# One expert at a time on both column halves of TensorE: sums in PSUM, 20 MB of landing room, 2 MB transfers with 16 KB runs

## What is computed

```python
def moe(h, w_router, b_router, w_up, b_up, w_down, b_down):
    logits = (x @ w_router + b_router)
    top_vals, top_idx = lax.top_k(logits, TOP_K)             # 4 of 32
    combine = jnp.sum(one_hot(top_idx, N_EXPERTS) * softmax(top_vals)[..., None], axis=1)

    def expert(acc, xs):
        wu, bu, wd, bd, g = xs                               # wu 1024 x 2048, wd 1024 x 1024
        gu = x @ wu + bu
        gate, up = gu[:, :D_FF], gu[:, D_FF:]
        gate = jnp.minimum(gate, SWIGLU_LIMIT)
        up = jnp.clip(up, -SWIGLU_LIMIT, SWIGLU_LIMIT)
        glu = gate * jax.nn.sigmoid(SWIGLU_ALPHA * gate)
        y = ((up + 1.0) * glu) @ wd + bd
        return acc + g[:, None] * y, None
```

## Time and profile before

| | |
|---|---|
| median of 3 runs | 1152.67 us (1152.51, 1152.67, 1154.61) |
| profiled execution | span 1150.5 us from its first to its last instruction; the time around its span is not recorded for it; the median of the runs is 2.2 us above this span |
| moved | 459.15 MB, mean 399 GB/s |
| TensorE matmul busy | 1054.2 us (92%) |
| VectorE, ScalarE, GpSimd busy | 331.5, 176.1, 55.6 us |
| granted TensorE clock, mean | 0.985 |

### The profile page before, as it was taken

The page is one execution under the profiler, slowest core; times in us unless marked ns, Lnnn a source line. Parts: engine busy times, 40 slices in busy tenths (PEclk is TensorE's granted clock), DMA queues, the critical chain, the costliest instruction groups (busy, mean ns, idle before and its releaser), DMA issues.

```text
span 1150.5 us, 13989 instructions
## 1 busy us (share of the span) xinstructions
PE 1054.2 (92%) x5718; PEld 518.3 (45%) x5718; DVE 331.5 (29%) x613; ACT 176.1 (15%) x319; POOL 55.6 (5%) x92
## 2 busy tenths in 40 slices
PE   7999999999999999989899998989898989898986
PEld 6987699834434343424243433333434333343422
DVE  4675877412213112111120202120212121212125
ACT  4453145401101010101010101010101010000011
POOL 5050000300000000000000000000000000000000
PEclk9999999999999999999999999999999999999999
DMA  9988987799999999999999999999999999999995
GB/s 309 376 247 334 385 289 311 281 419 428 427 400 428 427 429 428 428 428 429 428 429 428 428 428 428 428 429 428 429 428 428 429 428 428 428 427 424 421 420 212
DMA packets 58658, 459.15 MB, mean 399 GB/s; under 512 B 4804, under 2 KB 17160, under 8 KB 28056
## 3 DMA queue, kind: packets, MB, share of 16 engines
q1 hardware_dynamic: 57256, 455.12, 95.6%
q0 software_dynamic: 1168, 2.81, 1.0%
q10 hardware_dynamic: 192, 0.66, 0.2%
HBM read 456.99 MB, written 1.57 MB: 399 GB/s over the span
## 4 chain that ended last, share of the span: by engine, by line
PE 61%; DMA 33%; DVE 2%; SPq 2%; issue 1%; ACT 1%; DVEq 0%; ACTq 0%
DMA ring<-in_w_down_dram 30%; PE ps L1862 17%; PE ps L1877 10%; PE ps L1798 6%; PE ps L1751 5%; PE ps L1762 5%; PE ps L1447 3%; DMA ring<-in_w_in_dram 2%; PE ps L1897 2%; PE ps L1791 1%; PE ps L1778 1%; DMA ring<-in_w_ada_dram 1%; PE ps L1504 1%; PE ps L1505 1%; PE ps L1673 1%
## 5 line engine op out<-in xcount | busy, mean ns | idle before, releaser
L1862 PE MATMUL ps<-ring,arena 128*64 128x512 f32 x1664 | 364.5, 593 | 14.6 <-DMA ring<-in_w_up_dram 14.5
L1877 PE MATMUL ps<-ring,arena 128*64 128x512 f32 x896 | 210.8, 626 | 54.6 <-DMA ring<-in_w_down_dram 54.6
L1862 PEld LDWEIGHTS ps<-ring,arena 128*64 128x64 f32 x1664 | 121.0, 137 | 241.6 <-issue 239.2
L1877 PEld LDWEIGHTS ps<-ring,arena 128*64 128x64 f32 x896 | 72.5, 144 | 192.6 <-issue 173.5
L1305 DVE TENSOR_TENSOR arena<-ps,arena 128x512 f32<-128x512 f32 x64 | 44.3, 692 | 299.0 <-PE ps L1762 299.0
L1286 DVE TENSOR_SCALAR arena<-ps 128x512 f32<-128x512 f32 x32 | 20.6, 686 | 255.7 <-PE ps L1862 217.4
L1798 PE MATMUL ps<-ring,arena 128*64 128x512 f32 x368 | 81.1, 594 | 1.4 <-DVE arena L1288 0.7
L1751 PE MATMUL ps<-arena 128*128 128x128 f32 x512 | 63.7, 282 | 0.0
L1751 PEld LDWEIGHTS ps<-arena 128*128 128x128 f32 x512 | 61.7, 196 | 2.8 <-issue 2.8
L858 ACT ACTIVATE arena<-arena 128x512 f32<-128x512 f32 x32 | 19.6, 629 | 268.5 <-DVE arena L1286 268.4
L1762 PE MATMUL ps<-arena 128*128 128x512 f32 x128 | 57.8, 594 | 1.2 <-ACT arena L871 1.2
(11 more groups left out here) (281 smaller groups left out, 955.4 us busy)
## 6 DMA issues: line engine op xcount, KB each, us to landing
ring<-in_w_up_dram SPq DMA_DIRECT2D x127, 2048.0 KB, 26.9
ring<-in_w_down_dram SPq DMA_DIRECT2D x63, 2048.0 KB, 23.0
ring<-in_w_ada_dram SPq DMA_DIRECT2D x16, 1024.0 KB, 10.4
ring<-in_w_ada_dram SPq DMA_DIRECT2D x16, 512.0 KB, 10.1
ring<-in_w_in_dram SPq DMA_DIRECT2D x16, 512.0 KB, 9.5
ring<-in_w_in_dram SPq DMA_DIRECT2D x8, 1024.0 KB, 7.4
ring<-in_w_out_dram SPq DMA_DIRECT2D x4, 1024.0 KB, 6.8
ring<-in_w_pb_dram SPq DMA_DIRECT2D x2, 1024.0 KB, 8.2
```

What stands on the lines that cost most here:

```text
L1862: ins = mm(ps[CAP * a:CAP * a + CAP, n, :], xgT[:, h, kk, CAP * a:CAP * a + CAP], w[a][:, n * HALF:(n + 1) * HALF], start=False, stop=(kk ...
L1877: ins = mm(ps[CAP * a:CAP * a + CAP, YB + n, :], hT[:, f, CAP * a:CAP * a + CAP], w[a][:, n * HALF:(n + 1) * HALF], start=(f == 0), stop=( ...
```

## The change

The kernel after works on one expert at a time. Column half `h` of TensorE takes half of the hidden columns in the up projection (`up_row`, with a moving operand that takes 4 of every 8 floats) and column half `n` takes half of the output columns in the down projection (`down_rows`). So PSUM bank 0 holds the gate and bank 1 the up half for one expert; bank 2 the down output, bank 3 transposes, and banks 4 to 7 the sum over all experts, to which each `scatter` adds, with `start=False`. The residual is put into these banks first (`inject`), and the gated down bias with the first scatter; the modulation gate `gtf` is multiplied in before the scatter (`gated`). `acc`, `spare`, `yb`, `keep_busy` and the transposes of `x2T` go. Both experts of a pair are still gathered together: one half of the gather in each expert's step. `gather` reads `h2` at a step of 4 floats, before 2.

Landing room: four places of 4 MB in `ring` (`QUADS`) for the up weights of two experts, and `down_buf`, 4 MB in `arena`, for the down weights of one: 20 MB instead of 16 (and `spare`). Every transfer is 2 MB with 16 KB runs, except the last down's, which is cut into five. `moe_free` counts 4 for each up and 2 for each down. The slots of the stage ahead are renamed, in the same order; `wrt`, `selrow` and `rt` share a tile `late`. The copy of the modulation gate is four copies of half the partitions instead of two; ScalarE issues four loads for the down bias instead of one.

The core of the diff (on the TensorE side the removed functions are those printed above, and only the new ones are shown from `turn_hidden` on):

```diff
...
-    w_up_v = A_w_up[0].rearrange("e (c p j) n -> e p c (j n)", p=P, j=2)
-    w_down_v = A_w_down[0].rearrange("e (c p j) n -> e p c (j n)", p=P, j=4)
+    w_up_v = A_w_up[0].rearrange("e (c p j) n -> e p c (j n)", p=P, j=4)
+    w_down_v = A_w_down[0].rearrange("e (p j) n -> e p (j n)", p=P)
...
-        def pair_slot(n):
-            at = ORDER[n % RING]
-            return ring[:, at:at + 2, :].rearrange("p a b -> p (a b)")
+        def up_chunk(e, c):
+            at = QUADS[2 * (e % 2) + c]
+            return ring[:, at:at + 4, :]
...
+        xgT = region(0, 2, KB, P)
+        oh = region(4096, 2, P)
+        wo = region(4352, 2, 2, CAP)
+        woT = region(4608, 2, P)
+        down_buf = region(4864, KB, D)
+        gate = x[:, 0, 0:HALF]
+        sig = x[:, 0, HALF:D]
+        hid = x[:, 1, 0:HALF]
+        hT = x[:, 1, HALF:D].rearrange("p (a b) -> p a b", a=4)
+        bdn = x[:, 1, HALF:D]
+        yg = late[:, :].rearrange("p (a b) -> p a b", a=2)
+        gate_rows = gtf[:, :, 0:HALF]
+        gfin = gtf[:, :, HALF:D]
 
...
+        YB, TB, XB = 2, 3, 4
...
+                R = r * PIECES
+                if r:
+                    sp.wait_ge(moe_free, R)
+
+                def up_part(e, c, h):
+                    sp.dma_start(up_chunk(e, c)[:, 2 * h:2 * h + 2, :].rearrange("p a b -> p (a b)"),
+                                 w_up_v[e, :, c, 2 * h * SLOT:2 * (h + 1) * SLOT])\
+                        .then_inc(up_loaded[2 * (e % 2) + c][h], 16)
+
+                def down_part(e, j0, j1, loaded):
+                    sp.dma_start(down_buf[:, j0:j1, :].rearrange("p a b -> p (a b)"),
+                                 w_down_v[e, :, j0 * D:j1 * D]).then_inc(loaded, 16)
+
+                def up_whole(e, parity, c, after):
+                    for h in range(2):
+                        sp.wait_ge(moe_free, after + (h - 1))
+                        sp.dma_start(up_chunk(parity, c)[:, 2 * h:2 * h + 2, :].rearrange("p a b -> p (a b)"),
+                                     w_up_v[e, :, c, 2 * h * SLOT:2 * (h + 1) * SLOT])\
+                            .then_inc(up_loaded[2 * parity + c][h], 16)
+
+                def down_whole(e, after):
+                    for h in range(2):
+                        sp.wait_ge(moe_free, after + (h - 1))
+                        down_part(e, 4 * h, 4 * h + 4, down_loaded[h])
+
+                first_free = [(O_done, 1), (kv_stored, 32), (unit_ready, 24), (unit_ready, 24), (br_done, KB),
+                              (unit_ready, 28), (unit_ready, 32), (out_done, KB)]
+                order = [(0, 0, 0), (0, 0, 1), (0, 1, 0), (0, 1, 1), (1, 1, 1), (1, 0, 1), (1, 0, 0), (1, 1, 0)]
+                for (s, count), part in zip(first_free, order):
+                    if r == 0:
+                        sp.wait_ge(s, count)
+                    up_part(*part)
+                if r == 0:
+                    sp.wait_ge(logit_done, 2)
+                for h in range(2):
+                    down_part(0, 4 * h, 4 * h + 4, down_loaded[h])
+                for h in range(2):
+                    sp.wait_ge(moe_free, R + freed(0) + h + 1)
+                    up_part(2, 0, h)
+                up_whole(2, 0, 1, R + freed(0) + 4)
+                up_whole(3, 1, 0, R + freed(1) + 2)
+                up_whole(3, 1, 1, R + freed(1) + 4)
+                down_whole(1, R + freed(1) + 6)
+                up_whole(4, 0, 0, R + freed(2) + 2)
+
+                def steady(e, parity, at):
+                    down_whole(e, at + 6)
+                    up_whole(e + 2, parity, 1, at + 4)
+                    up_whole(e + 3, 1 - parity, 0, at + 8)
+
+                with sp.Fori(0, LOAD_LOOPS) as i:
+                    e0 = sp.snap(i * LOAD_BODY + 2)
+                    at0 = sp.snap(i * (6 * LOAD_BODY) + (R + freed(2)))
+                    for h in range(LOAD_BODY):
+                        steady(e0 + h, h, at0 + 6 * h)
+                e = 2 + LOAD_LOOPS * LOAD_BODY
+                steady(e, 0, R + freed(e))
+                down_whole(E - 3, R + freed(E - 3) + 6)
+                for h in range(2):
+                    sp.wait_ge(moe_free, R + freed(E - 3) + 3 + h)
+                    up_part(E - 1, 1, h)
+                sp.wait_ge(moe_free, R + freed(E - 2) + 5)
+                down_part(E - 2, 0, 4, down_loaded[0])
+                sp.wait_ge(moe_free, R + freed(E - 2) + 6)
+                down_part(E - 2, 4, 6, down_loaded[1])
+                down_part(E - 2, 6, 8, tail_loaded[0])
+                sp.wait_ge(moe_free, R + freed(E - 2) + 2)
+                last = up_chunk(E - 2, 0).rearrange("p a b -> p (a b)")
+                for n, (j0, j1) in enumerate(((0, 2), (2, 4), (4, 6), (6, 7), (7, 8))):
+                    sp.dma_start(last[:, j0 * D:j1 * D], w_down_v[E - 1, :, j0 * D:j1 * D])\
+                        .then_inc(tail_loaded[1 + n], 16)
...
+            def gated(g, used):
+                dve.wait_ge(moe_free, used)
+                dve.wait_ge(scat_done, g + 1)
+                for t in range(2):
+                    V.tensor_tensor(yg[:, t, :], ps[:, YB, :], gate_rows[:, t, :], ALU.mult).then_inc(yg_ready, 1)
+
+            def step(e, g, n, p, at):
+                if e % 2 == 0 and e < E - 2:
+                    dve.wait_ge(gath_done, g + 2)
+                    one_hots(p, (e // 2 + 1) % 2, n)
+                weighted(e, g)
+                swiglu(g, at + 4)
+                if e:
+                    gated(g - 1, at + 6)
...
+            def inject(t, n):
+
+                for j in range(4):
+                    ins = mm(ps[:, XB + 2 * t + n, j * P:(j + 1) * P], x2T[:, 4 * n + j, t * P:(t + 1) * P], ident[:, :],
+                             start=(j == 0), stop=False)
+                return ins
+
...
+            inject(0, 0)
...
+            def bias(g):
+
+                pe.wait_ge(u_read, g + 1)
+                pe.wait_ge(sel_ready, g + 1)
+                both = bparts[:, :].rearrange("q (g p j) -> q g p j", g=2, j=8)
+                for half in range(2):
+                    for h in range(2):
+                        mm(ps[CAP * h:CAP * h + CAP, half, :].rearrange("q (p j) -> q p j", j=4), selbuf[:, :],
+                           both[:, half, :, 4 * h:4 * h + 4], start=True, stop=False)
+
+            def up_row(e, kk):
+
+                place, a = (e // 2 + 1) % 2, e % 2
+                w = up_chunk(e, kk // 4)[:, kk % 4, :].rearrange("q (g p j) -> q g p j", g=2, j=8)
+                for half in range(2):
+                    for h in range(2):
+                        ins = mm(ps[CAP * h:CAP * h + CAP, half, :].rearrange("q (p j) -> q p j", j=4),
+                                 xgT[:, place, kk, CAP * a:CAP * a + CAP], w[:, half, :, 4 * h:4 * h + 4],
+                                 start=False, stop=(kk == KB - 1))
+                return ins
+
...
+            def turn_hidden(g):
+
+                pe.wait_ge(hid_ready, g + 1)
+                pe.wait_ge(woT_ready, g + 1)
+                for j in range(4):
+                    ins = tp(ps[:, TB, j * P:(j + 1) * P], gate[:, j * P:(j + 1) * P], ident[:, :])
+                ins.then_inc(hT_done, 1)
+
+            def scatter(g, done, each=0, last=False):
+
+                pe.wait_ge(woT_ready, g + 2)
+                for t in range(2):
+                    pe.wait_ge(yg_ready, g * 2 + (3 + t))
+                    for n in range(2):
+                        rows = slice(CAP * n, CAP * n + CAP)
+                        ins = mm(ps[:, XB + 2 * t + n, :], woT[rows, t, :], yg[rows, t, :], start=False, stop=last)
+                    if each:
+                        ins.then_inc(done, 1)
+                if not each:
+                    ins.then_inc(done, 1)
+
+            def down_rows(w, j0, j1):
+
+                for jj in range(j0, j1):
+                    h, j = jj // 4, jj % 4
+                    for n in range(2):
+                        ins = mm(ps[CAP * n:CAP * n + CAP, YB, :], hT[:, j, CAP * h:CAP * h + CAP],
+                                 w[:, jj, n * HALF:(n + 1) * HALF], start=(jj == 0), stop=(jj == KB - 1))
                 return ins
 
+            def down(e, g, loads):
+
+                pe.wait_ge(hTe_ready, g + 1)
+                pe.wait_ge(yg_ready, g * 2 + 2)
+                w = down_buf if e < E - 1 else up_chunk(E - 2, 0).rearrange("p a (c b) -> p (a c) b", c=2)
+                j0 = 0
+                for s, count, j1 in loads:
+                    pe.wait_ge(s, count)
+                    for lo, hi in ((0, 4), (4, 8)):
+                        a, b = max(j0, lo), min(j1, hi)
+                        if a < b:
+                            ins = down_rows(w, a, b)
+                            if b == hi:
+                                ins.then_inc(moe_free, 1)
+                    j0 = j1
+
+            def up(e, g, laps, r, first=False):
+
+                R = r * E
+                if not first:
```

(40 more changed lines are left out.)

791 lines of the change are left out of this document (252 added, 539 removed).

## The result

The changed kernel needs 1162.74 us (median of 4 runs, 1162.16 to 1165.09) against 1152.59 in the same comparison: 1.0090 times the time before, 95% interval 1.0075 to 1.0104, so 0.9% slower. Measured once more, unedited, it needed 1164.58 us and 1.0102 (1.0085 to 1.0119). The forecast was 1156.6, slower. The sign was right, and so was the place where most of the time would go, the hole behind expert 0. The amount was near that of the rival in which the gather's weights load slowly (1164.1).

A forecast was written before the change was run, and what follows sets the result against it. A stream of transfers was taken to bound the middle: 178 pieces at 4.896 us from 259.7 end near 1133.2; with 9.85 of tail and 11.4 of final chain 1154.4, plus 2.2 for the median, 1156.6 us. Range 1150.2 to 1167.

The forecast's parts named there:

- the hole behind expert 0: Transfers stop after the first expert, from 251.0 to 259.7 us, while TensorE works through expert 0 alone: 8.6 us.
- the rival in which the gather's weights load slowly: Gather's load doubles at a step of 4 floats: start slips 1.9, hole grows 3.8, nothing in steady state; 1164.1 us, chance 0.10.
- Work of a steady expert: TensorE's time per expert in the middle, gather 1.89 us included: 26.0 us, under 29.4 of transfer.
- Landing room: At the start, ten pieces landed by 230.8 us, before 8.6: worth 1.4 pieces, 7 us gained.
- All 16 KB runs: In the stream, 25 pieces no longer have 8 KB runs, 0.1 us each: 2.5 us gained.
- the second freed piece: In the stream before 251.0 us, waiting for the second piece that TensorE gives back makes one hole of 0.6 us.
- `down_buf` single: At the third down, the reload of the single buffer waits for the down before it: 0.8 us more.
- Up block and scatter: In each expert, the up block's strided moving operand costs nothing, and scatter products run two at once, scatter 1.87 us.
- Both rivals: Up block's moving operand reads slowly, 1167 to 1515 us, chance 0.08; scatter halves don't overlap, 1163.4, sharing the slow gather's 0.10.
- Rate in the middle: The stream of transfers in the middle stays at 428 GB/s, 4.896 us a piece.
- the rival of a faster stream: Transfers exceed 428 GB/s without half-filled runs and with two more pieces in flight: 1150.3 us at 431.3 GB/s, chance 0.14.
- Tail: At the end, TensorE finishes the last down 9.85 us after the bytes, then a final chain of 11.4 us.

The follow-up runs named there:

- two_rows: Changed kernel with the up weights brought as two rows per partition, so the gather reads `h2` at a step of two floats: 1157.2 us, ratio 1.0035.
- up_8k: Changed kernel with up-weight transfers made of two 8 KB runs per partition, 1 MB apart, and a packed gather: ratio 1.0102.
- overlap_first: Changed kernel with bias and three rows of expert 1's up block ahead of expert 0's turn: 0.7 to 2.1 us faster than the changed kernel's two measurements.
- fill_only: Changed kernel with pair 2's gather and the first scatter ahead of expert 0's turn: 0.8 us faster than its first measurement, 2.2 than its second.
- hold_down: Changed kernel with the tenth piece issued only when the first up piece is used: 2.2 us slower than its first measurement, 0.8 than its second.

## Why the prediction was right in sign and short in size

*The gather, 1.89 us a time in "Work of a steady expert": the term that was mis-sized.* It took 3.73 us for 16 records (3.94 at the start) and TensorE's expert 27.93 us, not 26.0. The rival priced this at 7.5 us; putting the step back gave 7.0 (ratios of 1.0075 to 1.0119 against 1.0021 to 1.0049). With the step of two the kernel needs 1157.2 us; the forecast, which assumed that load, was 1156.6. The rival's time was near, in part by luck: the parts that it names, 1.9 for the start and 3.8 for the hole, make 5.7 us and so 1162.3, and no term stands behind the other 1.8. Its "nothing in steady state" holds from 330 us on. What it lacks are the two other holes: 2.7 us of stream missing at 236 to 240, where two_rows has 426 GB/s, and 2.9 between 298 and 310, against 1.1 in two_rows between 292 and 304. What I gave 0.10 stood in the text with a page's rule for it (the Trainium skill, SBUF — State Buffer, "Door 1: The DMA port swizzle"): fewer than two reads per 16-byte line cost extra. The trace of before could not show it, since its step of 2 makes two reads. Four rows now agree: 195 ns packed, 199 at a step of 2, 328 and 329 at a step of 4. The same note of the Trainium skill goes on to say that one can stride for free as far as 4 fp32. Read as a step of four, that does not fit these rows, and the measurement decides. For a shape that no row has, the rule deserved at least even odds.

*Landing room, 7 us gained.* Ten pieces had landed near 232, not 230.8: an estimate from the eleventh, behind which the bytes stop at about 237, less 4.9. From 220 to 228 the stream moved at 377 GB/s, 430 before; why is open. The later holes took the head start back, and holding one piece changed little.

*All 16 KB runs, 2.5 us gained.* This holds. The changed kernel has 421 GB/s at 1110 to 1130 and two_rows 419, which looks as if the 418 of the kernel before belonged to the place. But not every transfer has 16 KB runs there: the second half of expert 30's down, in two pieces, and the last down, in five, have runs of 8 KB or less. Up to 1120 the changed kernel is at 428 (1100 to 1120), from 1120 to 1138 at 404. The kernel before runs at 420 in both stretches of its 8 KB pieces, so 25 of them cost about 2.3 us (25 x 4.896 x 8/420), and up_8k shows the cost by its time.

*The hole behind expert 0, 8.6 us.* 7.5, from 254.6 to 262. TensorE's idle time was 3.3 us, not 4.5: the sigmoid's table load ran at 241.92 beside the up block. `read_flags` cost nothing, since the bias follows the scatter directly. These savings, 2.2 us, paid for the slow gather in this place (1.9). Ahead of it I had given the second freed piece 0.6 us of a hole; it was 2.7.

*`down_buf` single, 0.8 us.* About 2.3 us at 300 (180 GB/s for 4 us) and 2.9 with what follows it; with the fast gather 1.1, so the rest is TensorE's lateness.

*Up block and scatter.* 24 records in 5.15 us, 0.2146 each as before: this moving operand, four neighbouring floats of every eight, costs nothing. Scatter 1.92 to 1.99 for 8 records of 64 rows: the halves overlap. Both rivals fall.

*Rate in the middle.* 428 as forecast; the rival of a faster stream falls.

*Tail, 9.85 us behind the bytes and 11.4 to the end.* 10.7 and 11.1. The bytes ended at 1138.6, 5.4 us later than forecast, and that is the miss: 2.3 of it are there when the hole behind expert 0 ends (262 instead of 259.7), some 2 come at 300, and the rest at the end of the stream, where the short pieces move at 404 GB/s.

## What to carry to other kernels

When a layout changes, price the access step of each operand of each instruction that reads it: fp32 at a step of four took 512 weight loads from 196 to 328 ns, and another split of the same rows gave transfers of the same size and runs with a step of two. A stream with no slack keeps each early hole to the end, so count the rate that is missing in the first stretch of each trace: here that one number moved with the time in most of the experiments. Fill a wait with work that depends on nothing the wait depends on; rows of the next expert looked free and brought a wait of their own. Before a rate is put down to a place or to a kind of transfer, look up in the code which transfers stand there.

## What the runs showed of the hardware that I had not expected

The pattern of a strided read counts: the up block's moving operand, four neighbouring floats of every eight, is read at full rate (0.2146 us a record), while the weight load of single floats at a step of four takes 328 ns instead of 196. A moving operand at that step was not run, so whether the two kinds of operand differ is open. VectorE read PSUM at a step of four floats at no cost (744 against 745 ns). Transfers of 2 MB with 8 KB runs moved at 420 GB/s, with 16 KB runs at 428. TensorE's granted clock fell to 0.50 behind the first gather in three executions with the slow gather (overlap_first, fill_only, hold_down), and 16 records took 5.35 us instead of 3.65; two executions of the changed kernel with the same gather showed no fall there. At expert 29's down 16 records took 5.37 us behind a wait of 2.5 us, and 3.65 behind one of 1.1.
